# Normalised activations of two inner norms: transposing products with a diagonal of the scales in place of plain transposes and a row product

## What is computed

```python
def _rmsnorm(x, g):
    x32 = x.astype(jnp.float32)
    y = x32 * lax.rsqrt(jnp.mean(x32 * x32, axis=-1, keepdims=True) + NORM_EPS)
    return y.astype(x.dtype) * g

def _modulate(x, shift, scale):
    return x * (1 + scale) + shift

u = _modulate(_rmsnorm(h, norm1_g[l]), sh1, sc1)
h = h + 0.5 * gt1 * _swiglu(u, ffn1_w_in[l], ffn1_w_out[l])
u = _modulate(_rmsnorm(h, norm2_g[l]), sh2, sc2)
h = h + gt2 * _hybrid_mixer(u, ...)
u = _modulate(_rmsnorm(h, norm3_g[l]), sh3, sc3)
h = h + 0.5 * gt3 * _swiglu(u, ffn2_w_in[l], ffn2_w_out[l])
return _rmsnorm(h, final_g)
```

## Time and profile before

| | us |
|---|---|
| median of 3 runs | 2132.74 (2130.19 to 2132.78) |
| the profiled execution, its own time | 2130.64 |
| its span, first to last instruction | 2128.9 |
| PE busy | 2092.2 (98%), 9563 records |
| DVE busy | 1508.4 (71%) |
| ACT busy | 1002.9 (47%) |

### The profile page before, as it was taken

How to read it: one execution, slowest core, us unless ns; L and a number is a source line. 1 busy time by engine, 2 the same in 40 slices (tenths; PEclk the granted TensorE clock), 3 DMA queues, 4 the chain that set the end, 5 groups by cost and what they waited for, 6 DMA issues and landing times.

```text
span 2128.9 us, 24008 instructions
## 1 busy us (share of the span) xinstructions
PE 2092.2 (98%) x9563; PEld 1729.1 (81%) x9563; DVE 1508.4 (71%) x1703; ACT 1002.9 (47%) x1261; POOL 4.6 (0%) x22
## 2 busy tenths in 40 slices
PE   6999999999999999999999999999999999999998
PEld 6888788888888878888888887878888888888886
DVE  6987987888788888786555889577555544555456
ACT  4676433443334455446555644554443344434444
POOL 0000000000000000000000000000000000000000
PEclk9999999999999999999999999999999999999999
DMA  9998898997899868875455678668655555566554
GB/s 361 387 375 302 314 321 323 327 335 275 307 337 327 285 227 316 315 247 170 159 160 161 239 286 311 207 211 299 221 179 193 189 190 194 182 198 195 182 176 158
DMA packets 249135, 539.70 MB, mean 254 GB/s; under 512 B 11584, under 2 KB 13888, under 8 KB 248384
## 3 DMA queue, kind: packets, MB, share of 16 engines
q1 hardware_dynamic: 248640, 538.04, 72.7%
q10 hardware_dynamic: 384, 0.13, 0.0%
HBM read 536.03 MB, written 2.10 MB: 253 GB/s over the span
## 4 chain that ended last, share of the span: by engine, by line
PE 91%; DVE 2%; ACT 1%; issue 1%; DMA 0%; ACTq 0%; DVEq 0%
PE pa L618 15%; PE pa L621 15%; PE pb L618 15%; PE pa L620 14%; PE pb L621 14%; PE pb L620 14%; PE px L633 1%; DVE lo L1489 1%; ACT hi L1058 0%; DVE ada_acc L1587 0%; PE pm L941 0%; PE px L701 0%; PE px L949 0%; DMA raw<-in_w_in_dram 0%; DVE hid_lo L1658 0%
## 5 line engine op out<-in xcount | busy, mean ns | idle before, releaser
L1489 DVE TENSOR_TENSOR lo<-raw,hi 128x1024 fp32r<-128x1024 f32 (+1 forms) x744 | 881.6, 1194 | 542.8 <-ACT hi L1058 542.1
L1058 ACT CAST hi<-raw 128x1024 fp32r<-128x1024 f32 (+1 forms) x744 | 762.4, 1028 | 1006.3 <-PE pa L621 496.9
L618 PE MATMUL pa<-hi,act_hi 128*128 128x512 f32 (+1 forms) x1056 | 413.8, 392 | 7.1 <-DVE act_lo L1556 4.5
L621 PE MATMUL pa<-hi,act_lo 128*128 128x512 f32 (+1 forms) x1056 | 408.4, 387 | 0.0
L620 PE MATMUL pa<-lo,act_hi 128*128 128x512 f32 (+1 forms) x1056 | 408.3, 387 | 0.0
L618 PE MATMUL pb<-hi,act_hi 128*128 128x512 f32 x1024 | 403.0, 394 | 0.0
L621 PE MATMUL pb<-hi,act_lo 128*128 128x512 f32 x1024 | 398.8, 389 | 0.0
L620 PE MATMUL pb<-lo,act_hi 128*128 128x512 f32 x1024 | 398.6, 389 | 0.0
L1587 DVE SCALAR_TENSOR_TENSOR ada_acc<-ada_w,cond,ada_acc 128x1024 f32<-128x1024 f32 (+1 forms) x240 | 275.2, 1147 | 6.4 <-DVE ada_acc L1587 0.5
L618 PEld LDWEIGHTS pa<-hi,act_hi 128*128 128x128 f32 x1056 | 198.6, 188 | 51.0 <-DVE act_lo L1556 5.6
L621 PEld LDWEIGHTS pa<-hi,act_lo 128*128 128x128 f32 x1056 | 198.6, 188 | 40.8
(11 more groups left out here) (286 smaller groups left out, 1335.7 us busy)
## 6 DMA issues: line engine op xcount, KB each, us to landing
raw<-in_ffn_w_in_dram SPq DMA_DIRECT2D x176, 1024.0 KB, 5.1
ada_w<-in_w_ada_dram SPq DMA_DIRECT2D x224, 512.0 KB, 6.0
raw<-in_ffn_w_out_dram SPq DMA_DIRECT2D x64, 1024.0 KB, 5.1
raw<-in_w_in_dram SPq DMA_DIRECT2D x64, 1024.0 KB, 5.1
ada_s<-in_w_ada_dram SPq DMA_DIRECT2D x64, 512.0 KB, 9.9
raw<-in_ffn_w_out_dram SPq DMA_DIRECT2D x32, 768.0 KB, 4.4
raw<-in_w_out_dram SPq DMA_DIRECT2D x16, 1024.0 KB, 5.8
raw<-in_w_att_up_dram SPq DMA_DIRECT2D x8, 1024.0 KB, 5.0
```

What stands on the lines that cost most here:

```text
L618: pe.matmul(ps, a_hi[:, k0 + kk, tok], w_hi, start=start and kk == 0, stop=False, skip_group_check=on)
L621: mm = pe.matmul(ps, a_lo[:, k0 + kk, tok], w_hi, start=False, stop=stop and kk == n - 1, skip_group_check=on)
L1058: act.copy(hi[:, (2 * j + half) % 4, 0:n, 0:w], raw[:, j % RING, 2 * half:2 * half + n, 0:w])\
L1489: dve.tensor_tensor(lo[:, j % RING, s, 0:w], raw[:, j % RING, s, 0:w], hi[:, (2 * j + half) % 4, 0:n, 0:w].bitcast(F32), ALU.subtract)\
```

## The change

Transposes (`h_turn`) and the row of scales (`norm_row`) go. In their place `norm_turn` multiplies a 128x128 block of `h` (stationary) by the diagonal `dg[:, tt, :]` (moving): the product is the block transposed and scaled per token. It is issued by the same ten pieces, all of them at or behind the boundary: pieces 0 and 1 first, 2 and 3 ahead of half unit 1, and from then on piece p + 2 ahead of the unit of piece p. Three PSUM banks take turns (both of `px`, and `pr`). ScalarE takes a piece out of PSUM with gain and shift at once (`norm_affine`, fp32 into `n_t`), and VectorE casts the high part and subtracts for the rest (`norm_split`, for all pieces). `last_gated` and `last_added` of token tile 0 move ahead of unit 1's `split` on VectorE, and `half_rstd(n, 0)` ahead of `last_gated` of token tile 1.

```diff
@@ -321,12 +321,10 @@
         h_half = sem("h_half")
         pv_ok = sem("pv_ok")
         ht_mm = sem("ht_mm")
-        ht_ok = sem("ht_ok")
         nt_t = sem("nt_t")
         nt_hi = sem("nt_hi")
         nt_lo = sem("nt_lo")
         gain_ok = sem("gain_ok")
-        rms_row = sem("rms_row")
         xt_mm = sem("xt_mm")
         xt_f = sem("xt_f")
         xt_hi = sem("xt_hi")
@@ -692,32 +690,33 @@
                     pe.matmul((pr, pm)[q % 2][:, :], ones[:, :], gt_row[:, q * NC:(q + 1) * NC],
                               start=True, stop=True).then_inc(gt_mm, 1)
 
-            def h_turn(n, g):
-
-                if g >= 2:
-                    pe.wait_ge(ht_ok, 8 * (n - 1) + g - 1)
+            def norm_turn(n, piece):
+
+                g, tts = PIECES[piece]
+                if piece < 4:
+                    pe.wait_ge(diag_ok, 2 * n + tts[0])
+                if piece == 0:
+                    pe.wait_ge(gt_ok, 4 * n)
+                if piece >= 3:
+                    pe.wait_ge(nt_t, 10 * (n - 1) + piece - 2)
+                bank = (px[:, 0, :], px[:, 1, :], pr[:, :])[piece % 3]
                 for k in (0, 1):
-                    for tt in range(TT):
-                        mm = pe.transpose(px[:, g % 2, k * T + tt * P:k * T + (tt + 1) * P],
-                                          h[:, tt, (2 * g + k) * P:(2 * g + k + 1) * P], ident[:, :])
+                    for tt in tts:
+                        mm = pe.matmul(bank[:, k * T + tt * P:k * T + (tt + 1) * P],
+                                       h[:, tt, (2 * g + k) * P:(2 * g + k + 1) * P], dg[:, tt, :],
+                                       start=True, stop=True)
                 mm.then_inc(ht_mm, 1)
 
-            def norm_row(n, tt):
-
-                pe.wait_ge(diag_ok, 2 * n + tt)
-                pe.wait_ge(gt_ok, 4 * n)
-                pe.matmul(pr[:, tt * P:(tt + 1) * P], ones[:, :], dg[:, tt, :], start=True, stop=True)\
-                    .then_inc(rms_row, 1)
-
             def norm_units(ph, n):
 
-                norm_row(n, 0)
-                pe.wait_ge(h_ok, H_BLOCKS[n] + 4)
-                h_turn(n, 6)
-                h_turn(n, 7)
+                norm_turn(n, 0)
+                norm_turn(n, 1)
                 for piece, (g, tts) in enumerate(PIECES[:4]):
                     if piece == 1:
-                        norm_row(n, 1)
+                        norm_turn(n, 2)
+                        norm_turn(n, 3)
+                    if piece >= 2:
+                        norm_turn(n, piece + 2)
                     pe.wait_ge(nt_lo, 10 * (n - 1) + piece + 1)
                     unit(ph, 0, 0, g, 2 * g, 2, act_hi, act_lo, pa, g == 0, False, tts=tts)
 
@@ -740,6 +739,8 @@
                         step(n_)
                     if norm and n_ < 2:
                         continue
+                    if norm and n_ < 6:
+                        norm_turn(norm, n_ + 4)
                     if norm and n_ < 8:
 
                         pe.wait_ge(nt_lo, 10 * (norm - 1) + n_ + 3)
@@ -764,10 +765,6 @@
                         if b == 0 and k0 <= 4 * (kn - 1) < k0 + n:
 
                             pe.wait_ge(nat_lo, 2 * (nat_last + 1))
-                        if norm and norm < 3 and b > 0 and (j, half) == (2, 0):
-                            pe.wait_ge(h_ok, H_BLOCKS[norm] + b)
-                            h_turn(norm, 2 * b - 2)
-                            h_turn(norm, 2 * b - 1)
                         if norm and b == 3 and (j, half) >= last[0][:2]:
                             if (j, half) == last[0][:2]:
                                 for tt in range(TT):
@@ -1089,15 +1086,6 @@
                                          accum_out=ss4[:, tt, b:b + 1])
                 ins.then_inc(ss_ok, 1)
 
-            def h_evac(n, g):
-
-                act.wait_ge(ht_mm, 8 * (n - 1) + g + 1)
-                act.wait_ge(gain_ok, 8 + n)
-                for k in (0, 1):
-                    ins = act.activation(n_t[:, 2 * g + k, :], px[:, g % 2, k * T:(k + 1) * T], ACT.Identity,
-                                         scale=gain[:, 2 * g + k:2 * g + k + 1])
-                ins.then_inc(ht_ok, 1)
-
             def out_phase(ph, kn, nat_last, gate=None, sq=None, norm=0):
                 for b in range(4):
                     for n_, (j, half, k0, n) in enumerate(units(4, kn)):
@@ -1110,9 +1098,6 @@
                                 act.copy(gt_row[:, q * NC:(q + 1) * NC], (pr, pm)[q % 2][:, :]).then_inc(gt_ok, 1)
                         if b > 0 and n_ == 5 and sq is not None:
                             squares(sq + b, b - 1)
-                        if b > 0 and n_ == 7 and norm:
-                            h_evac(norm, 2 * b - 2)
-                            h_evac(norm, 2 * b - 1)
 
             def turn_affine(g, count, scale, bias):
                 act.wait_ge(xt_mm, count + 1)
@@ -1146,15 +1131,20 @@
                 act.activation(st[:, 2, tt:tt + 1], ss4[:, tt, 3:4], ACT.Sqrt, scale=1.0 / D, bias=st[:, 0, tt:tt + 1])\
                     .then_inc(rt_ok, 1)
 
-            def norm_hi(n, sh, piece):
+            def norm_affine(n, sh, piece):
 
                 g, tts = PIECES[piece]
                 tok = slice(tts[0] * P, (tts[-1] + 1) * P)
-                act.wait_ge(nt_t, 10 * (n - 1) + piece + 1)
-                for kt in (2 * g, 2 * g + 1):
-                    ins = act.activation(act_hi[:, kt, tok], n_t[:, kt, tok], ACT.Identity,
+                act.wait_ge(ht_mm, 10 * (n - 1) + piece + 1)
+                if piece == 0:
+                    act.wait_ge(gain_ok, 8 + n)
+                bank = (px[:, 0, :], px[:, 1, :], pr[:, :])[piece % 3]
+                for k in (0, 1):
+                    kt = 2 * g + k
+                    ins = act.activation(n_t[:, kt, tok], bank[:, k * T + tts[0] * P:k * T + (tts[-1] + 1) * P],
+                                         ACT.Identity, scale=gain[:, kt:kt + 1],
                                          bias=mod[:, sh * KD + kt:sh * KD + kt + 1])
-                ins.then_inc(nt_hi, 1)
+                ins.then_inc(nt_t, 1)
 
             def final_scale(tt):
 
@@ -1170,13 +1160,12 @@
                     root_table()
                     half_root(n, 0)
                 if n_ == 2:
+                    norm_affine(n, sh, 0)
                     half_root(n, 1)
-                    for piece in (1, 2, 3, 4):
-                        norm_hi(n, sh, piece)
-                if n_ in (3, 4):
-                    h_evac(n, n_ + 3)
-                if 3 <= n_ < 8:
-                    norm_hi(n, sh, n_ + 2)
+                    for piece in (1, 2, 3):
+                        norm_affine(n, sh, piece)
+                if 2 <= n_ < 8:
+                    norm_affine(n, sh, n_ + 2)
 
             def first_body(ph):
 
@@ -1611,37 +1600,15 @@
                                                 bada[qs, cols], ALU.add)
                     ins.then_inc(mod_ok, 1)
 
-            def norm_t(n, piece):
+            def norm_split(n, piece):
 
                 g, tts = PIECES[piece]
-                tok = slice(tts[0] * P, (tts[-1] + 1) * P)
-                dve.wait_ge(ht_ok, 8 * (n - 1) + g + 1)
-                dve.wait_ge(rms_row, 2 * (n - 1) + tts[-1] + 1)
-                t = n_t[:, 2 * g:2 * g + 2, tok]
-                row = pr[:, tok].unsqueeze(1).broadcast_to([P, 2, len(tts) * P])
-                dve.tensor_tensor(t, t, row, ALU.mult).then_inc(nt_t, 1)
-
-            def norm_hi(n, sh, piece):
-
-                g, tts = PIECES[piece]
-                tok = slice(tts[0] * P, (tts[-1] + 1) * P)
+                part_ = (slice(None), slice(2 * g, 2 * g + 2), slice(tts[0] * P, (tts[-1] + 1) * P))
                 dve.wait_ge(nt_t, 10 * (n - 1) + piece + 1)
-                for kt in (2 * g, 2 * g + 1):
-                    ins = dve.tensor_scalar(act_hi[:, kt, tok], n_t[:, kt, tok],
-                                            mod[:, sh * KD + kt:sh * KD + kt + 1], None, ALU.add)
-                ins.then_inc(nt_hi, 1)
-
-            def norm_lo(n, sh, piece):
-
-                g, tts = PIECES[piece]
-                tok = slice(tts[0] * P, (tts[-1] + 1) * P)
+                dve.tensor_copy(act_hi[part_], n_t[part_]).then_inc(nt_hi, 1)
                 dve.wait_ge(nt_hi, 10 * (n - 1) + piece + 1)
-                for kt in (2 * g, 2 * g + 1):
-                    ins = dve.scalar_tensor_tensor(out=act_lo[:, kt, tok], in0=n_t[:, kt, tok],
-                                                   scalar=mod[:, sh * KD + kt:sh * KD + kt + 1],
-                                                   in1=act_hi[:, kt, tok].bitcast(F32),
-                                                   op0=ALU.add, op1=ALU.subtract)
-                ins.then_inc(nt_lo, 1)
+                dve.tensor_tensor(act_lo[part_], n_t[part_], act_hi[part_].bitcast(F32), ALU.subtract)\
+                    .then_inc(nt_lo, 1)
 
             def gate_row(gate, qs):
 
@@ -1820,28 +1787,19 @@
 
```

(21 more changed lines are left out.)

## The result

| | before | changed |
|---|---|---|
| median of 18 runs each, us | 2132.36 (2129.96 to 2133.1) | 2136.03 (2134.48 to 2138.48) |
| ratio | | 1.0020, 95% interval 1.0014 to 1.0027 |
| profiled execution, us | 2130.64 | 2135.94 |
| its span | 2128.9 | 2134.2 |

The account below looks back on a forecast made before the run. TensorE was taken as the bound; -4.35 (transposes), -0.9 (start), +5.4 (to unit 2) and +6.8 (units 3 to 5) gave +7.0 on 2130.64, so 2137.6. With 2139.7 from the median, 2138.6 was taken, range 2134 to 2142.8.

Parts of the forecast that it names:

- The bound and the sign: Whole kernel: TensorE sets the time and the change makes it slower, +7.0 us; chance of slower 0.80.
- Transposes taken out: Output projections: 0.87 us back at five of six places, none at block 3 of `ffn1_out2`; -4.35 us.
- Start of the first half unit: Boundary of each norm: first half unit starts earlier, -0.8 us at norm 2, some 0.1 at norm 1; together -0.9.
- Price of a group: Between units on TensorE: four products by the diagonal, 8 records, take 1.03 us, and 0.10 behind them.
- No wait in the ladder: First half unit to unit 2: 9.96 us of half units and groups with no wait, +5.4 us over both norms.
- Not slower: Rival: products slip under neighbours' loads and drains, group about 0.49 us, total 2131; chance 0.17 within 0.2%, 0.03 faster.
- the prediction's own signs of being wrong: At the norms: groups under 0.84 us, norm 2's first half unit over 1.5 us earlier, or waits for `act_lo`.
- slower by over 0.2%: Whole kernel: slower by more than 4.3 us, given 0.80 in all, 0.6 of it for the forecast itself.
- Four transposes' price per product: Rival, groups at the norms: a product costs 0.396 us instead of 0.234, +9 more, 2147.7; chance 0.03.
- A waiting ladder: Rival, both norms: late second diagonal or turns waiting for a bank, half a microsecond at four places, +4, 2142.6; chance 0.1.
- projections that give nothing back: Rival, output projections: another engine is behind at blocks 1 and 2 too, +4.35 us at most, 2143; chance 0.07.

Follow-up runs that it names:

- the second of the three looks: The kernel before, run again unchanged for its granted clock: 2132.50 us.
- the doubled groups: The changed kernel with every product by the diagonal issued twice into the same place: 2147.57 us, ratio 1.0074.
- the three filled kernels: Unread products in TensorE's boundary idle: kernel before 2130.61 us, changed kernel 2134.22, and a mix (diagonal products for pieces 0 to 3, transposes elsewhere) 2128.35.

## Why the prediction was right

**The bound and the sign** held: TensorE sets the time, the products are twice the records of the transposes, and they moved from a place where the transposes cost 0.87 us per pair of groups to one where each group has its own delay.

**Transposes taken out**: forecast -4.35, measured -4.4. Five of six places gave 0.88 or 0.89 back, and block 3 of `ffn1_out2` left the bare wait of 0.95 as told.

**Start of the first half unit**: -0.8 forecast and -0.68 measured at norm 2, -0.1 and 0.0 at norm 1. The reordering alone does not do it (4.11 us); with the short first piece it does (3.70).

**Price of a group**: this is the term that was mis-sized, and it explains the forecast's excess. "A group of four products (8 records) so takes 0.33 + 6 x 0.117 = 1.03 us, and 0.10 behind it." It took 0.81, and 0.08 to 0.09 behind it. The 0.117 per record was near (0.10 to 0.11). The 0.33 was not the price of two records: most of the excess in it was a wait for VectorE. The product behind that row product needs `act_lo` of piece 1, and VectorE in the kernel before ends it at 1388.08 + 0.61 = 1388.69, 0.05 us ahead of the product's start at 1388.74:

```profile
1388.08 0.61 DVE L1640 SCALAR_TENSOR_TENSOR act_lo<-n_t,mod,act_hi 128x128 fp32r<-128x128 f32 x2
```

In the second of the three looks, the same kernel, that `act_lo` ends at 1389.82, ahead of the row product, and the row product delays its unit by 1390.51 - 1390.37 = 0.14 us:

```profile
1389.21 0.61 DVE L1640 SCALAR_TENSOR_TENSOR act_lo<-n_t,mod,act_hi 128x128 fp32r<-128x128 f32 x2
...
1390.37 0.38 PE L709 MATMUL pr<-dg,ones 128*128 128x128 f32 x2
1390.51 0.47 PE L618 MATMUL pa<-hi,act_hi 128*128 128x512 f32 x1
```

So 2, 4, 8 and 16 records between such units delay them by 0.14, 0.35, 0.81 and 1.70 us, and with the 0.09 behind them that is 0.11 us a record in each case. With 0.14 in place of 0.33 the prediction's own sum would have come to +7.0 - 14 x 0.19 = +4.3. The group's price of 0.90 in place of 1.13 takes 3.2 us off in all, nearly the whole gap between +7.0 and +3.6; the start gave 0.2 less than forecast, the transposes 0.1 more, and the small steps elsewhere 0.4. The eight transposes taken out, as many records as four products and between the same neighbours, delayed their unit by 0.79 us, and that was the nearer row.

**No wait in the ladder**: right. From half unit to unit 2 at full clock 4 x 1.46 + 4 x 0.81 = 9.1 against 9.14 measured, and the page names no further wait of TensorE there.

**The rivals.** Not slower needed a group of 0.84 for "within 0.2%", and it came to 0.81, so one of the prediction's own signs of being wrong was met: the trace's own sum, 3.6, lies under 4.3 and the difference of medians (3.67) too, while the ratio's 4.3 lies on the line. The sign and the range held, and the range held because it was drawn down to 2134, into this rival; the size of the change was put nearly twice too large, and the case of "slower by over 0.2%" was given too much. Four transposes' price per product is excluded: 0.81 against 0.35 is 2.3 times. The Trainium skill's factor of four for FP32 (TensorE: Matmul & The Clock Gate, Terms) is not what these 128-column operands show; by it, with the 0.35 of four transposes, a group would take 1.4 us and the change cost 14 x 0.59 = 8 us more. A waiting ladder and projections that give nothing back are excluded by the rows above.

**What the forecast lacked** is the clock: it took the full clock of one execution for granted. That the difference of the medians (3.67) still agrees with the sum at full clock (3.6) is luck in part: both kernels have executions with half clock at the norms, and it costs them unlike amounts (0.8 to 0.9 us a norm in the kernel before, 1.4 to 2.7 in the changed one).

## What to carry to other kernels

Price a short group of products by its records, from a group of about the same length between the same neighbours, and not from the shortest one at hand. Before a delay is taken as an instruction's price, look when the follower's operands were ready: here 0.19 of 0.33 us was a wait for another engine, too short to be marked as idle time. Where one engine is the bound, use the costly form (a product that transposes and scales in one) only in the gap where latency counts, and the cheap form (a plain transpose) where the engine is busy; a transfer of work that lightens engines with room is worth nothing. And look at more than one execution: a gap of the matrix engine can be followed by half clock in some of them, and a few idle products in the gap can buy it back.

## What the runs showed of the hardware

The granted clock behind the same gap differed from execution to execution: 1.00 at both norms in one profile of the kernel before, 0.50 to 0.53 at both in another. The work in half clock took 0.43 us per product of 512 columns instead of 0.227. With 1.3 us (kernel before) to 1.7 us (the other two) of products put into the gap's idle time no profile of the three filled kernels showed it at the norms; of the eight profiles without such products and without the doubled groups, five did. The Trainium skill (TensorE: Matmul & The Clock Gate, Part 1) says that the throttled state is the default and that activity releases it; the filled and unfilled runs agree, in so far as three profiles against eight and the spreads (1.3, 1.5 and 1.4 us against 4.0, 3.6 and 4.1) can tell. What decides between two executions of the same kernel was not tried.
